# A decoder layer in split fp32: inputs stored back to front, and the two halves of each weight side by side

## The chip, the cores and the metric

The kernel runs on one core of one Trainium2 chip. The metric is device time in microseconds (us), the median of the runs shown; three runs of the kernel before gave 2773.8, 2774.07 and 2774.15 us.

## What is computed

One layer of a hybrid recurrent decoder, for 256 prompt tokens and 32 sample tokens (8 sequences of 4) together, so T = 288 columns in every product. Cut to what matters here:

```
h    = rmsnorm(x)
proj = h @ w_in                      # 2048 -> z | xBC | dt | q | f | i | g | gates
y_a  = grouped_rmsnorm(ssd(conv(xBC), dt) * silu(z)) @ w_br_a      # 4096 -> 2048
y_b  = (rmsnorm(hgrn2(q, f, i)) * silu(g)) @ w_br_b                # 2048 -> 2048
x    = x + rmsnorm((sigmoid(ga) * y_a + sigmoid(gb) * y_b) @ w_out)
x    = x + rmsnorm(relu(rmsnorm(x) @ w_up)^2 @ w_down)             # 2048 -> 8192 -> 2048
x    = x + sigmoid(rmsnorm(x) @ w_ple_gate) * (p @ w_ple_proj)
```

All is in fp32. The outputs are x and the new recurrent and convolution states.

## The kernel before

Everything stands with features on the 128 partitions and the 288 tokens along the free axis. The weights of all large products come from DRAM as 772 slabs of 512 KB in the order in which they are used. A slab is 8 blocks of 128x128 (SK = 8): one output tile of 128 features, and 8 of the 128-feature tiles of the input.

A slab passes four stations. SyncE loads it into one of four slots of `raw` (RING = 4). ScalarE rounds it to the reduced-precision type fp32r into `w_hi` (`split_hi`, L508). VectorE subtracts what was rounded from the whole and puts the rest into `w_lo` (`split_lo`, L1024). TensorE then multiplies (`multiply`, L1665 to L1667): for each of the 8 blocks three matmuls of 288 columns, w_hi with the input's high part, w_hi with its low part, and w_lo with its high part, all summed in one PSUM bank. So a slab is 24 matmuls, each with its own load of a 128x128 weight block. `multiply_pair` (L1681 to L1683) does the same for two output tiles at once where a normalised input is only just being made, and the loop at L2065 to L2067 for the small projection of p.

The splits run three slabs ahead of the matmuls (AHEAD = 3): calls of `ahead` stand between the other instructions of ScalarE and VectorE, by hand, one for each slab that TensorE multiplies. The waits are: ScalarE for the load (`raw_in`) and for the slot to be free of matmuls (`slab_used`), VectorE for `hi_done`, TensorE for `lo_done`, and SyncE's next load into the slot for `lo_done`.

Each input of a product is split in the same way, one or several tiles of 288 columns at a time, into fp32r tiles: h_hi and h_lo (the normalised x, made three times: L533 and L1061, then twice L889 and L1515), o (L633, L1239), y (L801, L1452), m (L826, L1464), u (L897, L1564) and p (L958, L1605). A tile is 1152 bytes of each partition, and the tiles of an input follow one another. The buffers h_hi, o_hi, y_hi, u_hi and m_hi start 480 bytes past a multiple of 512 (`aligned` does this for the first four).

The stages in order, with their slabs: HGRN, 16 heads of 8 slabs (128); the branch projection with its gate (64); SSD, 8 groups of 20 slabs (160); the other branch projection with its gate (96); the output product (32); the feed-forward (256); the last projection and gate (4 and 32). In HGRN and SSD, TensorE, VectorE and ScalarE also have the recurrences to do, between the slabs. In HGRN, `level` gives views of two halves of pairs at seven distances: for distance 1 its operands take every second element.

Lines of the prediction's steps: L1190, L1191, L1216 and L1217 (VectorE on views of `level`), L1146 and L1150 (a product and a reduction in HGRN, once a head; the reduction steps over 64 elements), L1411 (once a group of SSD), L1941 (TensorE, 128-column products in SSD).

```
raw = sb("raw", [P, RING, SK, P])
w_hi = sb("w_hi", [P, RING, SK, P], F32R)
w_lo = sb("w_lo", [P, RING, SK, P], F32R)
...
        for h in LEVELS:                                     # 64, 32, 16, 8, 4, 2, 1
            c4 = level(hcum, 0, h)                           # "p (b a j) -> p b a j", a=2, j=h
            e4 = level(he, LOFF[h], h)
            ...
            V.tensor_tensor(e4[:, :, 1, :], c4[:, :, 1, :], ref, ALU.subtract)
            V.tensor_tensor(e4[:, :, 0, :], ref, c4[:, :, 0, :], ALU.subtract)
```

Of the kernel before, what the change touches and what calls it, by code (L numbers as in the profile page):

```python
# [30 lines left out]
P = 128  # L31
# [115 lines left out]
def layer_program(nc, io):  # L147
# [353 lines left out]
    def _(act):  # L501
        def split_hi(m, k):

            act.wait_ge(raw_in[k], (m + 1) * 16)
            if not (isinstance(m, int) and m == 0):

                act.wait_ge(slab_used, m * RING + (k + 1 - RING))
            nc.scalar.activation(w_hi[:, k], raw[:, k], ACT.Copy).then_inc(hi_done, 1)  # L508

# [21 lines left out]
        for c in range(NC):  # L531
            act.wait_ge(n_xn, 2 * c + 2)
            nc.scalar.activation(h_hi[:, 2 * c:2 * c + 2], hn32[:, 2 * c:2 * c + 2],  # L533
                                 ACT.Copy).then_inc(n_hi, 1)
            if c in (1, 4):
                split_hi(0, (c + 2) // 3)
# [34 lines left out]
        def hgrn(it, first, gemm):  # L571
# [60 lines left out]
            if not first:  # L632
                nc.scalar.activation(tile_at(o_hi, r), one(hso[:, :]), ACT.Copy).then_inc(hg_ohi, 1)  # L633
            nxt(7)
# [165 lines left out]
        def y_hi_chunk(c):  # L800
            nc.scalar.activation(y_hi[:, 4 * c:4 * c + 4], y32[:, 4 * c:4 * c + 4], ACT.Copy).then_inc(y_his, 1)  # L801

# [21 lines left out]
        def merged_hi(t):  # L824
            act.wait_ge(ga_m, t + 1)
            nc.scalar.activation(tile_at(m_hi, t), one(aya[:, :]), ACT.Copy, scale=0.5).then_inc(ga_hi, 1)  # L826

# [67 lines left out]
        def up_hi_part(t, tt):  # L895
            act.wait_ge(up_sq, tt + 1)
            nc.scalar.activation(tile_at(u_hi, t), one(tmp[:, :]), ACT.Copy).then_inc(up_hi, 1)  # L897

# [58 lines left out]
        act.wait_ge(p_land, 16)  # L957
        nc.scalar.activation(p_hi[:, :, :], p_in[:, :, :], ACT.Copy).then_inc(p_his, 1)  # L958
        down(0, True, 1)
# [58 lines left out]
    def _(dve):  # L1018
        V = nc.vector

        def split_lo(m, k):

            dve.wait_ge(hi_done, m * RING + (k + 1))
            V.tensor_tensor(w_lo[:, k], raw[:, k], w_hi[:, k].bitcast(F32), ALU.subtract).then_inc(lo_done, 1)  # L1024

# [33 lines left out]
        def normalised_lo(c):  # L1059
            dve.wait_ge(n_hi, c + 1)  # L1060
            V.tensor_tensor(h_lo[:, 2 * c:2 * c + 2], hn32[:, 2 * c:2 * c + 2],  # L1061
                            h_hi[:, 2 * c:2 * c + 2].bitcast(F32), ALU.subtract).then_inc(n_lo, 1)
# [69 lines left out]
        def hgrn(it, first, gemm):  # L1132
# [104 lines left out]
            if not first:  # L1237
                dve.wait_ge(hg_ohi, it)
                V.tensor_tensor(tile_at(o_lo, it - 1), one(hso[:, :]), tile_at(o_hi, it - 1).bitcast(F32),  # L1239
                                ALU.subtract).then_inc(hg_olo, 1)  # L1240
# [209 lines left out]
        for c in range(8):  # L1450
            dve.wait_ge(y_his, c + 1)
            V.tensor_tensor(y_lo[:, 4 * c:4 * c + 4], y32[:, 4 * c:4 * c + 4],  # L1452
                            y_hi[:, 4 * c:4 * c + 4].bitcast(F32), ALU.subtract).then_inc(y_los, 1)
            if c in (1, 3):
                ahead(U_GA, 2 * GA_SLABS, 0, 6 + c // 2)

        def merge(t):
            dve.wait_ge(evac, t * 2 + (T_GA + 2))
            dve.wait_ge(ga_in, t * 16 + 16)
            V.scalar_tensor_tensor(aya[:, :], atg[:, :], 1.0, aya[:, :], ALU.add, ALU.mult).then_inc(ga_t, 1)  # L1460
            dve.wait_ge(ga_t, t + 1)
            V.tensor_tensor(aya[:, :], aya[:, :], amb[:, :], ALU.add).then_inc(ga_m, 1)
            dve.wait_ge(ga_hi, t + 1)
            V.scalar_tensor_tensor(tile_at(m_lo, t), one(aya[:, :]), 0.5, tile_at(m_hi, t).bitcast(F32),  # L1464
                                   ALU.mult, ALU.subtract).then_inc(ga_lo, 1)
# [91 lines left out]
        def up_tile(t, j, half):  # L1557
# [5 lines left out]
            dve.wait_ge(up_hi, tt + 1)  # L1563
            V.tensor_tensor(tile_at(u_lo, t), one(tmp[:, :]), tile_at(u_hi, t).bitcast(F32),  # L1564
                            ALU.subtract).then_inc(up_lo, 1)
# [38 lines left out]
        dve.wait_ge(p_his, 1)  # L1604
        V.tensor_tensor(p_lo[:, :, :], p_in[:, :, :], p_hi[:, :, :].bitcast(F32), ALU.subtract).then_inc(p_los, 1)  # L1605
        down(0, True, 1)
# [48 lines left out]
    def _(pe):  # L1655
        M = nc.tensor

        def multiply(m, k, out, hi, lo, kt0, first, last, chunks=None):


            pe.wait_ge(lo_done, m * RING + (k + 1))
            for i in range(SK):
                if chunks is not None and i % chunks[1] == 0:
                    pe.wait_ge(chunks[0], (kt0 + i) // chunks[1] + 1)
                M.matmul(out, w_hi[:, k, i], hi[:, kt0 + i], start=first and i == 0, stop=False)  # L1665
                M.matmul(out, w_hi[:, k, i], lo[:, kt0 + i], start=False, stop=False)  # L1666
                op = M.matmul(out, w_lo[:, k, i], hi[:, kt0 + i], start=False, stop=last and i == SK - 1)  # L1667
            op.then_inc(slab_used, 1)

        def multiply_pair(fu, s0, kt0, first, last, banks, chunk0):  # L1670
# [6 lines left out]
            for i in range(SK):  # L1677
                if i % 2 == 0:
                    pe.wait_ge(n_lo, chunk0 + (kt0 + i) // 2 + 1)
                for k, out in zip(slots, (banks[0][:, 0:T], banks[1][:, 0:T])):  # L1680
                    M.matmul(out, w_hi[:, k, i], h_hi[:, kt0 + i], start=first and i == 0, stop=False)  # L1681
                    M.matmul(out, w_hi[:, k, i], h_lo[:, kt0 + i], start=False, stop=False)
                    op = M.matmul(out, w_lo[:, k, i], h_hi[:, kt0 + i], start=False, stop=last and i == SK - 1)  # L1683
                    if i == SK - 1:
# [367 lines left out]
        for s in range(4):  # L2052
            m, k = slab(U_PROJ, 4, 0, s)
            pe.wait_ge(lo_done, m * RING + k + 1)
            for j in range(4):
# [7 lines left out]
                for i in range(2):  # L2063
                    w = 2 * j + i
                    M.matmul(out, w_hi[:, k, w], p_hi[:, i], start=i == 0, stop=False)  # L2065
                    M.matmul(out, w_hi[:, k, w], p_lo[:, i], start=False, stop=False)
                    op = M.matmul(out, w_lo[:, k, w], p_hi[:, i], start=False, stop=i == 1)  # L2067
                op.then_inc(pj_tile if j < 3 else slab_used, 1)
# [250 lines left out]
```

## Time and profile before

| what | value |
|---|---|
| median of three runs | 2774.07 us (2773.8 to 2774.15) |
| span of the profiled execution | 2770.1 us, 4.0 us under the median; its own whole time is not listed |
| PE (TensorE matmul) busy | 2709.0 us, 98% |
| DVE (VectorE) busy | 1787.1 us, 65% |
| ACT (ScalarE) busy | 1421.8 us, 51% |
| POOL (GpSimd) busy | 182.9 us, 7% |
| DMA | 484.22 MB, mean 175 GB/s |

The span runs from the first instruction to the last. Engines work side by side, so the busy times don't add up. Matmuls are pipelined and the end of each is modelled, so records of neighbouring matmuls overlap: the distance between starts tells the pace, not the length of one. PEld is TensorE's loading of weights, which overlaps the matmul before it. "Chain" is the chain of work that ended last, followed back from the last instruction. PEclk is the granted TensorE clock, 1.00 for 2.4 GHz and 0.50 for 1.2 GHz.

### The profile page before, as it was taken

What the parts mean: (1) busy time and instruction counts of PE and PEld (TensorE: products, weight loads), DVE (VectorE), ACT (ScalarE), POOL (GpSimd) and SP (SyncE); (2) the same over time, 40 slices, a digit from 0 to 9 for tenths busy, and PEclk for the clock granted to TensorE, in tenths of its full rate; (3) what the DMA queues carried; (4) which work ended last, traced back from release to release, by engine and by line L of the source; (5) the groups of instructions that cost most, each with busy time, mean ns of one, the idle gap of its engine ahead of it and who ended that gap; (6) DMA issues with size and microseconds to landing.
All of it is one profiled execution on the core that took longest, in us unless ns stands there. A gap on an engine that the chain in (4) does not pass through costs nothing.

```text
span 2770.1 us, 59417 instructions
## 1 busy us (share of the span) xinstructions
PE 2709.0 (98%) x22077; PEld 2639.3 (95%) x22077; DVE 1787.1 (65%) x3214; ACT 1421.8 (51%) x2285; POOL 182.9 (7%) x297
## 2 busy tenths in 40 slices
PE   6999999999999999999989999989999999999999
PEld 5999999999999999999989999989999999999989
DVE  7878787844378888888864444476543355654475
ACT  6666666643356556556643334454443344444363
POOL 0111111100011111111110000000000000000000
PEclk9999999999999999999999999999999999999999
DMA  4544454555556665665555556435554455554544
GB/s 170 176 161 161 163 175 157 165 179 177 172 203 207 199 209 200 210 204 202 191 174 179 174 169 209 164 119 175 164 173 165 162 166 167 164 170 162 165 132 160
DMA packets 135289, 484.22 MB, mean 175 GB/s; under 512 B 17248, under 2 KB 19696, under 8 KB 134080
## 3 DMA queue, kind: packets, MB, share of 16 engines
q1 hardware_dynamic: 114560, 410.88, 44.3%
q0 software_dynamic: 20672, 72.55, 8.2%
q8 instruction: 40, 0.66, 0.1%
q14 instruction: 17, 0.14, 0.0%
HBM read 449.58 MB, written 33.78 MB: 174 GB/s over the span
## 4 chain that ended last, share of the span: by engine, by line
PE 84%; DVE 9%; ACT 3%; issue 2%; DMA 1%; DVEq 0%; POOL 0%; ACTq 0%; POOLq 0%
PE acc L1667 25%; PE acc L1665 25%; PE acc L1666 24%; DVE w_lo L1024 2%; DVE ccv L1310 1%; ACT w_hi L508 1%; PE bank L1665 1%; PE bank L1667 1%; PE bank L1666 1%; PE bank L1846 1%; PE bank L1954 1%; PE bank L1778 1%; PE bank L1941 1%; PE bank L1863 0%; DVE x L1509 0%
## 5 line engine op out<-in xcount | busy, mean ns | idle before, releaser
L1024 DVE TENSOR_TENSOR w_lo<-raw,w_hi 128x1024 fp32r<-128x1024 f32 x772 | 937.9, 1223 | 604.2 <-ACT w_hi L508 599.3
L1665 PE MATMUL acc<-h_hi,w_hi 128*128 128x288 f32 x3872 | 1157.6, 299 | 11.7 <-DVE h_lo L1061 7.7
L1667 PE MATMUL acc<-h_hi,w_lo 128*128 128x288 f32 x3872 | 1148.4, 297 | 0.0
L1666 PE MATMUL acc<-h_lo,w_hi 128*128 128x288 f32 x3872 | 1131.1, 292 | 0.0
L508 ACT ACTIVATE w_hi<-raw 128x1024 fp32r<-128x1024 f32 x772 | 810.8, 1055 | 438.8 <-PE acc L1667 366.2
L1665 PEld LDWEIGHTS acc<-h_hi,w_hi 128*128 128x128 f32 x3872 | 728.5, 188 | 19.7 <-issue 7.4
L1666 PEld LDWEIGHTS acc<-h_lo,w_hi 128*128 128x128 f32 x3872 | 738.8, 191 | 2.8
L1667 PEld LDWEIGHTS acc<-h_hi,w_lo 128*128 128x128 f32 x3872 | 727.1, 188 | 0.0
L1667 PE MATMUL acc<-u_hi,w_lo 128*128 128x288 f32 x1024 | 303.6, 296 | 0.0
L1665 PE MATMUL acc<-u_hi,w_hi 128*128 128x288 f32 x1024 | 302.6, 296 | 0.0
L1666 PE MATMUL acc<-u_lo,w_hi 128*128 128x288 f32 x1024 | 298.5, 292 | 0.0
L1666 PEld LDWEIGHTS acc<-u_lo,w_hi 128*128 128x128 f32 x1024 | 195.2, 191 | 0.0
L1665 PEld LDWEIGHTS acc<-u_hi,w_hi 128*128 128x128 f32 x1024 | 192.4, 188 | 0.0
L1667 PEld LDWEIGHTS acc<-u_hi,w_lo 128*128 128x128 f32 x1024 | 191.8, 187 | 0.0
L1667 PE MATMUL acc<-y_hi,w_lo 128*128 128x288 f32 x384 | 113.9, 296 | 0.0
L1665 PE MATMUL acc<-y_hi,w_hi 128*128 128x288 f32 x384 | 113.5, 296 | 0.0
L1666 PE MATMUL acc<-y_lo,w_hi 128*128 128x288 f32 x384 | 111.9, 292 | 0.0
L1310 DVE SCALAR_TENSOR_TENSOR ccv<-craw,prh,ccv 128x312 f32<-128x312 f32 x144 | 78.3, 544 | 5.1
L1667 PE MATMUL acc<-m_hi,w_lo 128*128 128x288 f32 x256 | 75.9, 296 | 0.0
L1665 PE MATMUL acc<-m_hi,w_hi 128*128 128x288 f32 x256 | 75.6, 296 | 0.0
L1666 PE MATMUL acc<-m_lo,w_hi 128*128 128x288 f32 x256 | 74.6, 292 | 0.0
L1666 PEld LDWEIGHTS acc<-y_lo,w_hi 128*128 128x128 f32 x384 | 73.2, 191 | 0.0
(411 smaller groups left out, 3538.1 us busy)
## 6 DMA issues: line engine op xcount, KB each, us to landing
raw<-in_w SPq DMA_DIRECT2D x772, 512.0 KB, 3.3
ht<-in_ht POOLq DMA_DIRECT2D x64, 256.0 KB, 4.1
out_ssm_s<-ht POOLq DMA_DIRECT2D x64, 256.0 KB, 4.0
cbc<-cum_d POOLq DMA_DIRECT2D x8, 1152.0 KB, 6.8
hs<-in_s POOLq DMA_DIRECT2D x16, 512.0 KB, 4.6
out_hg_s<-hsn POOLq DMA_DIRECT2D x16, 512.0 KB, 5.0
x_in<-in_x SPq DMA_DIRECT2D x4, 576.0 KB, 5.9
mixb<-bmb POOLq DMA_DIRECT2D x16, 144.0 KB, 2.0
```

The source lines that it names most:

```text
L508: nc.scalar.activation(w_hi[:, k], raw[:, k], ACT.Copy).then_inc(hi_done, 1)
L1024: V.tensor_tensor(w_lo[:, k], raw[:, k], w_hi[:, k].bitcast(F32), ALU.subtract).then_inc(lo_done, 1)
L1310: op = V.scalar_tensor_tensor(ccv[:, 0:CVC], src[:, w:w + CVC], prh[:, c, w:w + 1], ccv[:, 0:CVC], ALU.mult, ALU.add)
L1665: M.matmul(out, w_hi[:, k, i], hi[:, kt0 + i], start=first and i == 0, stop=False)
L1666: M.matmul(out, w_hi[:, k, i], lo[:, kt0 + i], start=False, stop=False)
L1667: op = M.matmul(out, w_lo[:, k, i], hi[:, kt0 + i], start=False, stop=last and i == SK - 1)
L1778: M.matmul(b_diag[32 * q:32 * q + 32, 64 * n + 32 * b:64 * n + 32 * b + 32], ks, qs, start=True, stop=True)
L1846: op = M.matmul(bank[5][TS * b:TS * b + TS, :], cfd[:, TS * seq:TS * seq + TS], ht[:, b], start=half == 0, stop=True, skip_group_check=True)
L1941: op = M.matmul(bank[1][:, P * p:P * p + P], xw[:, b, P * p:P * p + P], bt[:, b], start=b == 0, stop=b == 1)
L1954: M.matmul(y[lo:lo + HD, 0:TP], xd[:, 0, HD * j:HD * j + HD], me[:, j, 0:TP], start=True, stop=True)
```

## The change

The high and low parts of a weight stand next to each other in one buffer, `w_split`: for each block of 128x128 the 128 columns follow at a step of two elements (8 bytes), high parts on the even places and low parts on the odd ones. The buffer takes the place of `w_hi` and `w_lo` and has their size together. Every split input tile is written with its 288 columns in the opposite order: the splits read their source from the last column to the first. The matmuls read these tiles from the last column to the first, so the products come out in the order that they had. No instruction is added or taken away, and no wait changes.

```diff
-    w_hi = sb("w_hi", [P, RING, SK, P], F32R)
-    w_lo = sb("w_lo", [P, RING, SK, P], F32R)
+    SLOT = 2 * SK * P
+    w_split = sb("w_split", [P, RING * SLOT], F32R)
+
+    def slot(k):
+
+        at = k * SLOT
+        return w_split[:, at:at + SLOT].rearrange("p (i n a) -> p i a n", i=SK, a=2)
+
+    w_hi = [slot(k)[:, :, 0] for k in range(RING)]
+    w_lo = [slot(k)[:, :, 1] for k in range(RING)]
...
-            nc.scalar.activation(w_hi[:, k], raw[:, k], ACT.Copy).then_inc(hi_done, 1)
+            nc.scalar.activation(w_hi[k], raw[:, k], ACT.Copy).then_inc(hi_done, 1)
...
-            V.tensor_tensor(w_lo[:, k], raw[:, k], w_hi[:, k].bitcast(F32), ALU.subtract).then_inc(lo_done, 1)
+            V.tensor_tensor(w_lo[k], raw[:, k], w_hi[k].bitcast(F32), ALU.subtract).then_inc(lo_done, 1)
...
-                op = nc.scalar.activation(h_hi[:, t], x2[:, t], ACT.Identity, scale=cols[:, col + t:col + t + 1])
+                op = nc.scalar.activation(h_hi[:, t], x2[:, t, ::-1], ACT.Identity, scale=cols[:, col + t:col + t + 1])
...
-                op = V.scalar_tensor_tensor(h_lo[:, t], x2[:, t], cols[:, col + t:col + t + 1],
+                op = V.scalar_tensor_tensor(h_lo[:, t], x2[:, t, ::-1], cols[:, col + t:col + t + 1],
...
-                M.matmul(out, w_hi[:, k, i], hi[:, kt0 + i], start=first and i == 0, stop=False)
-                M.matmul(out, w_hi[:, k, i], lo[:, kt0 + i], start=False, stop=False)
-                op = M.matmul(out, w_lo[:, k, i], hi[:, kt0 + i], start=False, stop=last and i == SK - 1)
+                M.matmul(out, w_hi[k][:, i], hi[:, kt0 + i, ::-1], start=first and i == 0, stop=False)
+                M.matmul(out, w_hi[k][:, i], lo[:, kt0 + i, ::-1], start=False, stop=False)
+                op = M.matmul(out, w_lo[k][:, i], hi[:, kt0 + i, ::-1], start=False, stop=last and i == SK - 1)
```

The other splits of inputs (o, y, m, u, p and the first h) and the matmuls of `multiply_pair` and of the small projection are changed in the same way.

## Rows read from the trace of the kernel before

**Rows 1.** The page: busy time by engine, and the chain by engine

```profile
PE 2709.0 (98%) x22077; PEld 2639.3 (95%) x22077; DVE 1787.1 (65%) x3214; ACT 1421.8 (51%) x2285; POOL 182.9 (7%) x297
...
PE 84%; DVE 9%; ACT 3%; issue 2%; DMA 1%; DVEq 0%; POOL 0%; ACTq 0%; POOLq 0%
```

**Rows 2.** The page's costliest groups: out<-in, shapes, xcount | busy us, mean ns | idle before

```profile
L1024 DVE TENSOR_TENSOR w_lo<-raw,w_hi 128x1024 fp32r<-128x1024 f32 x772 | 937.9, 1223 | 604.2 <-ACT w_hi L508 599.3
...
L508 ACT ACTIVATE w_hi<-raw 128x1024 fp32r<-128x1024 f32 x772 | 810.8, 1055 | 438.8 <-PE acc L1667 366.2
```

**Rows 3.** Waits of all engines: who <- whom, us in total, times, longest

```profile
DVE w_lo L1024 <- ACT w_hi L508: 599.3, 487, 2.8
ACT w_hi L508 <- PE acc L1667: 366.2, 232, 3.5
```

**Rows 4.** Busy time by stretch: us, PE, PEld, DVE, ACT, POOL (x instructions), PEclk, DMA, GB/s

```profile
60.00:460.00 400.00, 398.98 (x4378) 381.37 (x4378) 323.69 (x940) 268.09 (x452) 44.75 (x49) 1.00 0.49 166
...
700.00:1400.00 700.00, 691.90 (x5287) 656.59 (x5286) 551.97 (x1011) 405.06 (x834) 104.02 (x190) 1.00 0.60 200
```

**Rows 5.** Busy time by stretch, one of the feed-forward, where TensorE does slabs alone

```profile
2200.00:2400.00 200.00, 200.00 (x1515) 200.00 (x1514) 111.15 (x138) 88.04 (x117) 0.00 (x0) 1.00 0.51 165
```

**Rows 6.** Busy time by stretch, the first matmuls of the feed-forward

```profile
1823.82:1825.97 2.15, 2.15 (x10) 2.15 (x10) 2.12 (x5) 0.96 (x2) 0.00 (x0) 0.50 0.00 0
```

**Rows 7.** Timeline of PE in that stretch: start us, us, engine line operation

```profile
1823.82 0.44 PE L1682 MATMUL acc<-h_lo,w_hi 128*128 128x288 f32 x1
1824.06 0.44 PE L1683 MATMUL acc<-h_hi,w_lo 128*128 128x288 f32 x1
1824.30 0.44 PE L1681 MATMUL acc<-h_hi,w_hi 128*128 128x288 f32 x1
1824.54 0.44 PE L1682 MATMUL acc<-h_lo,w_hi 128*128 128x288 f32 x1
```

**Rows 8.** Timeline of PE in the output product: the first matmul of four tiles

```profile
1801.63 0.29 PE L1665 MATMUL acc<-m_hi,w_hi 128*128 128x288 f32 x1
...
1802.02 0.30 PE L1665 MATMUL acc<-m_hi,w_hi 128*128 128x288 f32 x1
...
1802.43 0.30 PE L1665 MATMUL acc<-m_hi,w_hi 128*128 128x288 f32 x1
...
1802.83 0.29 PE L1665 MATMUL acc<-m_hi,w_hi 128*128 128x288 f32 x1
```

**Rows 9.** Timeline of PEld in SSD: sixteen weight loads in a row

```profile
1060.00 1.89 PEld L1941 LDWEIGHTS bank<-bt,xw 128*128 128x128 f32 x16
```

**Rows 10.** Timeline of DVE in HGRN: `level` at distance 4, 2 and 1

```profile
113.05 0.28 DVE L1190 TENSOR_TENSOR he<-hcum 128x128 f32<-128x128 f32 x1
...
113.45 0.30 DVE L1190 TENSOR_TENSOR he<-hcum 128x144 f32<-128x144 f32 x1
...
113.89 0.30 DVE L1190 TENSOR_TENSOR he<-hcum 128x144 f32<-128x144 f32 x1
```

**Rows 11.** Timeline of DVE in HGRN: the product, and the reduction that steps over 64

```profile
101.33 0.56 DVE L1146 TENSOR_TENSOR hdm<-bank,consts 128x384 f32<-128x384 f32 x1
...
102.08 0.86 DVE L1150 TENSOR_REDUCE hab<-hdm 128x64 f32<-128x384 f32 x1
```

**Rows 12.** Groups by line and shape: the input splits at a norm

```profile
L889 ACT ACTIVATE h_hi<-x,cols 128x288 fp32r<-128x288 f32 x32 | 15.5, 539 | 18.0 <-DVE x L1509 18.0
...
L1515 DVE SCALAR_TENSOR_TENSOR h_lo<-x,cols,h_hi 128x288 fp32r<-128x288 f32 x32 | 15.1, 511 | 0.3 <-ACT h_hi L889 0.3
```

**Rows 13.** The chain by line, in HGRN (60 to 460 us)

```profile
by line: PE acc L1665 26.5%; PE acc L1667 26.1%; PE acc L1666 25.5%; PE bank L1778 3.1%; PE bank L1758 1.9%; PE bank L1765 1.7%; PE bank L1807 1.5%; PE bank L1771 1.4%; PE bank L1769 1.2%; PE bank L1797 1.0%; PE bank L1796 1.0%; PE bank L17
```

**Rows 14.** The chain by line, in SSD (700 to 1400 us)

```profile
by line: PE acc L1665 17.9%; PE acc L1667 17.4%; PE acc L1666 17.0%; issue 6.9%; DVE ccv L1310 5.4%; DVE w_lo L1024 4.7%; ACT w_hi L508 3.2%; PE bank L1954 2.3%; PE bank L1846 2.1%; PE bank L1941 2.0%; DVE ccv L1306 1.6%; ACT me L721 1.6%; 
```

**Rows 15.** Two lines' instructions: count, ns min/median/max, first and last start us

```profile
L1150 DVE TENSOR_REDUCE hab<-hdm x16: 847/856/859, 70.7 to 550.8; 128x64 f32<-128x384 f32 x16
...
L1411 DVE TENSOR_TENSOR cbm<-bank,consts x8: 557/557/559, 796.6 to 1353.1; 128x384 f32<-128x384 f32 x8
```

More of the change, by code:

```diff
@@ L532, in _ @@
             act.wait_ge(n_xn, 2 * c + 2)
-            nc.scalar.activation(h_hi[:, 2 * c:2 * c + 2], hn32[:, 2 * c:2 * c + 2],
+            nc.scalar.activation(h_hi[:, 2 * c:2 * c + 2], hn32[:, 2 * c:2 * c + 2, ::-1],
                                  ACT.Copy).then_inc(n_hi, 1)
@@ L632, in hgrn @@
             if not first:
-                nc.scalar.activation(tile_at(o_hi, r), one(hso[:, :]), ACT.Copy).then_inc(hg_ohi, 1)
+                nc.scalar.activation(tile_at(o_hi, r), one(hso[:, ::-1]), ACT.Copy).then_inc(hg_ohi, 1)
             nxt(7)
@@ L825, in merged_hi @@
             act.wait_ge(ga_m, t + 1)
-            nc.scalar.activation(tile_at(m_hi, t), one(aya[:, :]), ACT.Copy, scale=0.5).then_inc(ga_hi, 1)
+            nc.scalar.activation(tile_at(m_hi, t), one(aya[:, ::-1]), ACT.Copy, scale=0.5).then_inc(ga_hi, 1)
         for t in range(EARLY):
@@ L896, in up_hi_part @@
             act.wait_ge(up_sq, tt + 1)
-            nc.scalar.activation(tile_at(u_hi, t), one(tmp[:, :]), ACT.Copy).then_inc(up_hi, 1)
+            nc.scalar.activation(tile_at(u_hi, t), one(tmp[:, ::-1]), ACT.Copy).then_inc(up_hi, 1)
         def up(i, half, banks, done=0):
@@ L957, in _ @@
         act.wait_ge(p_land, 16)
-        nc.scalar.activation(p_hi[:, :, :], p_in[:, :, :], ACT.Copy).then_inc(p_his, 1)
+        nc.scalar.activation(p_hi[:, :, :], p_in[:, :, ::-1], ACT.Copy).then_inc(p_his, 1)
         down(0, True, 1)
@@ L1238, in hgrn @@
                 dve.wait_ge(hg_ohi, it)
-                V.tensor_tensor(tile_at(o_lo, it - 1), one(hso[:, :]), tile_at(o_hi, it - 1).bitcast(F32),
+                V.tensor_tensor(tile_at(o_lo, it - 1), one(hso[:, ::-1]), tile_at(o_hi, it - 1).bitcast(F32),
                                 ALU.subtract).then_inc(hg_olo, 1)
@@ L1463, in merge @@
             dve.wait_ge(ga_hi, t + 1)
-            V.scalar_tensor_tensor(tile_at(m_lo, t), one(aya[:, :]), 0.5, tile_at(m_hi, t).bitcast(F32),
+            V.scalar_tensor_tensor(tile_at(m_lo, t), one(aya[:, ::-1]), 0.5, tile_at(m_hi, t).bitcast(F32),
                                    ALU.mult, ALU.subtract).then_inc(ga_lo, 1)
@@ L1563, in up_tile @@
             dve.wait_ge(up_hi, tt + 1)
-            V.tensor_tensor(tile_at(u_lo, t), one(tmp[:, :]), tile_at(u_hi, t).bitcast(F32),
+            V.tensor_tensor(tile_at(u_lo, t), one(tmp[:, ::-1]), tile_at(u_hi, t).bitcast(F32),
                             ALU.subtract).then_inc(up_lo, 1)
@@ L1680, in multiply_pair @@
                 for k, out in zip(slots, (banks[0][:, 0:T], banks[1][:, 0:T])):
-                    M.matmul(out, w_hi[:, k, i], h_hi[:, kt0 + i], start=first and i == 0, stop=False)
-                    M.matmul(out, w_hi[:, k, i], h_lo[:, kt0 + i], start=False, stop=False)
-                    op = M.matmul(out, w_lo[:, k, i], h_hi[:, kt0 + i], start=False, stop=last and i == SK - 1)
+                    M.matmul(out, w_hi[k][:, i], h_hi[:, kt0 + i, ::-1], start=first and i == 0, stop=False)
+                    M.matmul(out, w_hi[k][:, i], h_lo[:, kt0 + i, ::-1], start=False, stop=False)
+                    op = M.matmul(out, w_lo[k][:, i], h_hi[:, kt0 + i, ::-1], start=False, stop=last and i == SK - 1)
                     if i == SK - 1:
@@ L2064, in _ @@
                     w = 2 * j + i
-                    M.matmul(out, w_hi[:, k, w], p_hi[:, i], start=i == 0, stop=False)
-                    M.matmul(out, w_hi[:, k, w], p_lo[:, i], start=False, stop=False)
-                    op = M.matmul(out, w_lo[:, k, w], p_hi[:, i], start=False, stop=i == 1)
+                    M.matmul(out, w_hi[k][:, w], p_hi[:, i, ::-1], start=i == 0, stop=False)
+                    M.matmul(out, w_hi[k][:, w], p_lo[:, i, ::-1], start=False, stop=False)
+                    op = M.matmul(out, w_lo[k][:, w], p_hi[:, i, ::-1], start=False, stop=i == 1)
                 op.then_inc(pj_tile if j < 3 else slab_used, 1)
```

8 lines of the change are left out of this document (4 added, 4 removed).

## The prediction

> **What bounds the kernel now.** The page first: TensorE's matmuls fill 98% of the span, VectorE 65%, ScalarE 51%, and the chain that ended last is 84% TensorE [rows 1]. Then the waits: VectorE's low split waits 599.3 us for ScalarE's high split, and that waits 366.2 us for matmuls to free a slot of the ring [rows 3]. So the splits stand ready and are held back by TensorE, not the other way round. By stretch: in the feed-forward TensorE does nothing but slabs, and VectorE is busy for 111 of 200 us [rows 5]. In HGRN VectorE is busy for 323.69 of 400 us, 81%, and in SSD for 551.97 of 700 us, 79% [rows 4]. There TensorE's work is still nearly the whole, but VectorE has only a fifth to spare.
>
> The pace of one matmul is the number that this change is about. In the feed-forward 1515 matmuls take 200.00 us: 132.0 ns each, with the granted clock at 1.00, its upper level of 2.4 GHz [rows 5]. The same instruction at the lower level, 1.2 GHz (granted 0.50), after TensorE had waited for the norm, starts every 0.24 us [rows 6, 7], three steps of exactly 0.72 us in all. That is 288 columns at one in a cycle, with nothing on top. Twice the clock should give 120 ns. So at full clock 12.0 ns of each matmul are spent on something that half the clock doesn't show: not an instruction's fixed cost in cycles, but data that come too late. Nor is the loss even: of three neighbouring tiles of the same product, three matmuls each, one takes 0.39, one 0.41 and one 0.40 us [rows 8], though only the place of the tile differs.
>
> What else reads then is the next weight block. Sixteen loads in a row take 1.89 us, of which the last 0.19 is one load's length; so a load follows a load in (1.89 - 0.19)/15 = 113 ns [rows 9]. While TensorE reads a tile of 1152 bytes in 120 to 132 ns, about 9 bytes a ns, it reads 512 bytes of weights in 113 ns, 4.5 bytes a ns. The inputs overtake the weights in the same memory several times in each matmul, and where the two readers want the same part of it, one waits. That is my reading; the rows show the loss, its dependence on pace and on place, not the cause.
>
> **The change, part by part.**
>
> Weights interleaved: a block now covers 1024 bytes for each part, so in the same 113 ns the weight reader walks at 1024/113 = 9.1 bytes a ns, as fast as the inputs. Inputs reversed and read downwards: both readers go the same way if the weights of a block are read from the last column to the first. Two readers of one speed and one direction keep their distance: they meet at the start at most, one gives way, and they don't meet again. No row shows the direction in which weights are read, so this is the step that decides.
>
> The gain per matmul has ends far apart. The best is all of 12.0 ns [rows 5, 7]. The other end is a loss: twice the bytes swept by the weight reader without the lock, twice the meetings, 12.0 ns more. I take 7 ns, a pace of 125: nearer to the 120 of half clock, since equal speeds are what the two edits together make, and short of it, since each load and each matmul starts anew.
>
> There are 772 splits [rows 2], so 772 slabs of 24 matmuls, 18,528.
> - 484 slabs lie outside HGRN and SSD, where TensorE sets the pace alone: 484 x 24 x 7 ns = 81.3 us.
> - HGRN, 128 slabs: 21.5 us. The three lines of slab matmuls are 78% of the chain there [rows 13], the rest mostly other matmuls, and VectorE's 81% would become 85%. I count nine tenths: 19.4 us.
> - SSD, 160 slabs: 26.9 us. The slab matmuls are only 52% of the chain, with VectorE's and ScalarE's lines between [rows 14]. I count six tenths, 16.1 us; what is late next there is VectorE's convolution and split.
>
> Sum: 117 us less.
>
> The splits, at a step of two elements: VectorE reads one operand and writes its result so, 772 times, 1.223 us each [rows 2]. `level` at distance 1 takes every second element in all three operands: 144 columns in 0.30 us, as at distance 2, where they come in pairs, and 128 columns in 0.28 [rows 10]. The difference of 0.02 us is that of 16 more columns. So the step costs nothing; this is nearly the form of the split, and I take 0. The upper end is a far step: 384 columns at a step of 64 take 0.86 us against 0.56 for a product of 384 [rows 11], 0.78 ns more a column, 0.80 us a split. ScalarE's high split (1.055 us [rows 2]) writes at that step, which no ScalarE row shows; bounds 0 and the same 0.80 us, no gain, since as many elements pass. I take 0, by the nearer row. What covers a small excess on either is the lead of three slabs, 3 x 24 x 132 ns = 9.5 us; it is gone where VectorE has no fifth to spare.
>
> The Vector Engine (DVE) Microarchitecture Reference of the Trainium skill (5.2, Measured stream behaviour on trn2) speaks against this edit: a port keeps its full rate only while its elements come in adjacent pairs. By that rule the split would lose its rate, and the sum would be that of the third rival below. The `level` rows disagree at this step, and they decide.
>
> The reversed reads: 178 tiles are split once each on ScalarE and VectorE, 0.54 and 0.51 us where a norm makes them [rows 12]. No row reads downwards. I take 0, as many bytes in the same order of lines; the upper end is 0.78 ns x 288 = 0.22 us a tile. For the 48 tiles of the three norms, where TensorE waits, that would be 2 x 48 x 0.22 = 21 us; the other 130 lie beside matmuls.
>
> No instruction, DMA or wait is added, and the queues of SP and POOL issue what they did. Faster slabs ask for loads sooner: 165 GB/s and half of the DMA engines' time [rows 5] become 174, which the 200 of SSD [rows 4] covers.
>
> So the span goes from 2770.1 to about 2653 us. With the 4.0 us by which the median stands above it, **2657 us**.
>
> **The rivals.**
> 1. **Twice the meetings (slower).** If weights are read upwards, or the parts of memory that collide are such that two equal streams stay together, the weight reader sweeps twice the bytes and the loss doubles: +12.0 ns x 18,528 = +222 us, 2996; with half of that, 2885. For it: 12 ns are lost already with a slow weight reader. Against: the speeds become equal. It decides on the slab matmuls, from a pace of 132.3 ns (0.3 ns x 18,528 = 5.6 us, 0.2%).
> 2. **The load becomes the bound (slower).** A step of 8 bytes may stretch the load itself. From 132/113 = 1.17 times its time it sets the pace. At 1.3 times, 147 ns: +15 x 18,528 = +278 us, 3052; at twice, 226 ns, over 4500. Against: the matmul reads twice as many columns in a ns as a load does.
> 3. **The splits become the bound (slower).** A head of HGRN takes (550.8 - 70.7)/15 = 32.0 us, a group of SSD (1353.1 - 796.6)/7 = 79.5 [rows 15]. With 0.80 us more a split, VectorE has 81% of 32.0 + 8 x 0.80 = 32.3 us of work a head, and 79% of 79.5 + 20 x 0.80 = 78.8 a group. At 95% busy that takes 34.0 and 82.9 us: 16 x 2.0 + 8 x 3.4 = 59 us more, 2833. Against: rows 10.
> 4. **No meeting at all (same).** If the 12 ns come from the input's read alone, its order and the weights' place change nothing: 2774. For it: no row shows a matmul at full clock without a load beside it. TensorE: Matmul & The Clock Gate of the Trainium skill (Part 2, step 1) says just this: two independent read ports, so loading weights takes nothing from the running matmul. It also states a pace of N/2.4 + 2.5 ns, 122.5 here; the trace has 132.0, so something that page leaves out is at work.
>
> That the change doesn't do what it says I leave out: each read and write follows from the views in the diff.
>
> **How the numbers follow.** My forecast, a gain of 7 ns or some other part of the 12: 0.65. The fourth rival and what comes out even: 0.10. Twice the meetings 0.17, the load 0.04, the splits 0.04: 0.25 together. If all 12 ns go, the same weights give 139 + 33 + 28 = 200 us, 2574. Within the forecast most lies from 2590 up, down to small gains. The range 2590 to 2850 leaves out the last bit of gain (0.05) and the slower cases beyond half of a doubling (0.14). Its likeliest part, the forecast's own, is 2590 to 2740. Faster by over 0.2% (about what a measurement of this kernel can tell from no change) 0.65, within it 0.10, slower 0.25.
>
> **What would show it.** Right: in the feed-forward 200 us hold some 1600 matmuls instead of 1515 at the same granted clock, neighbouring tiles differ by less, the splits stay at 1.223 and 1.055 us, and ScalarE waits less for a slot. The chain in SSD moves from slab matmuls to VectorE. Wrong: a pace above 132 ns (first rival), a weight load above its 0.19 us (second), a split near 2 us with TensorE waiting for `lo_done` (third), or a pace still at 132 (fourth).

## The result, and the profile after

The changed kernel takes 2780.8 us (median of 10 runs, 2778.9 to 2783.2) against 2773.8 us for the kernel before on the same chip: 1.0026 times as long, with a 95% interval of 1.0018 to 1.0035. That is slower by just over what a measurement can tell from no change. The profiled execution spans 2777.0 us against 2770.1.

First the page (busy time by engine, the chain by engine) and the two splits among the costliest groups, of the changed kernel:

```profile
PE 2710.8 (98%) x22077; PEld 2639.6 (95%) x22077; DVE 1790.3 (64%) x3214; ACT 1510.0 (54%) x2285; POOL 182.7 (7%) x297
...
PE 88%; DVE 6%; ACT 3%; issue 1%; DMA 1%; POOL 0%; DVEq 0%; ACTq 0%; POOLq 0%
...
L1032 DVE TENSOR_TENSOR w_split<-raw,w_split 128x1024 fp32r<-128x1024 f32 x772 | 941.0, 1226 | 627.8 <-ACT w_split L516 623.6
...
L516 ACT ACTIVATE w_split<-raw 128x1024 fp32r<-128x1024 f32 x772 | 904.0, 1179 | 405.6 <-PE acc L1675 336.8
```

Only one engine's work has grown: ScalarE's, from 1421.8 to 1510.0 us [rows 1]. It is the high split, 1.179 us where it was 1.055 [rows 2], 772 times 0.124 us. VectorE's split is unchanged: 1.226 us against 1.223, although it reads one operand and writes at a step of two.

Then busy time by stretch (us, PE, PEld, DVE, ACT and POOL with their instructions, granted clock, DMA share, GB/s), one stretch of the feed-forward and the whole of SSD:

```profile
2200.00:2400.00 200.00, 200.00 (x1514) 200.00 (x1514) 109.84 (x135) 95.73 (x116) 0.00 (x0) 1.00 0.51 165
700.00:1400.00 700.00, 688.21 (x5245) 651.20 (x5244) 546.50 (x1003) 419.66 (x832) 101.63 (x185) 1.00 0.59 198
```

The pace, the number the prediction was about, hasn't moved: 1514 matmuls in 200 us, where it was 1515 [rows 5]. (A stretch counts the two matmuls that its edges cut, so I take 2 off from here on: 200/1513 = 132.2 ns before, 200/1512 = 132.3 after. From first to last start in that stretch it is 132.22 ns in both kernels, and 12.2 ns over the 120, not 12.0.) SSD does 42 matmuls fewer in 700 us than before [rows 4].

Yet the change did something to the matmuls. This is TensorE's timeline in the output product, the first matmul of five neighbouring tiles:

```profile
1809.15 0.30 PE L1673 MATMUL acc<-m_hi,w_split 128*128 128x288 f32 x1
...
1809.55 0.30 PE L1673 MATMUL acc<-m_hi,w_split 128*128 128x288 f32 x1
...
1809.94 0.30 PE L1673 MATMUL acc<-m_hi,w_split 128*128 128x288 f32 x1
...
1810.34 0.30 PE L1673 MATMUL acc<-m_hi,w_split 128*128 128x288 f32 x1
...
1810.74 0.30 PE L1673 MATMUL acc<-m_hi,w_split 128*128 128x288 f32 x1
```

The tiles take 0.40, 0.39, 0.40 and 0.40 us, where they took 0.39, 0.41 and 0.40 [rows 8]. In the trace's starts, which are kept to the ns, every tile now has the same three steps, 135, 131 and 131 ns; before, steps ran from 127 to 138 and depended on the tile. The unevenness went, as forecast, if not for the forecast's reason alone (e11_few below). The mean stayed.

Last, one product of SSD that is made once a group (count, shortest, median and longest ns, first and last start):

```profile
L1419 DVE TENSOR_TENSOR cbm<-bank,consts x8: 557/558/558, 797.4 to 1359.0; 128x384 f32<-128x384 f32 x8
```

Before it ran from 796.6 to 1353.1 [rows 15]. So of the 6.9 us by which the span grew, 0.8 had come when this product of SSD's first group was reached, 5.1 came between the first and the last, and 1.0 behind it.

So there are two questions: what holds the pace at 132 ns whatever the layout, and what SSD lost.

### The profile page after: what moved, and what is told of

It is laid out like the page before. It is cut to its first block, busy times and chain, and to the rows that moved or that the text cites. A ratio compares the mean times of both kernels' runs of the same rounds, so it can differ in the third digit from the quotient of the medians.

```text
span 2777.0 us, 59417 instructions
## 1 busy us (share of the span) xinstructions
PE 2710.8 (98%) x22077; PEld 2639.6 (95%) x22077; DVE 1790.3 (64%) x3214; ACT 1510.0 (54%) x2285; POOL 182.7 (7%) x297
## 4 chain that ended last, share of the span: by engine, by line
PE 88%; DVE 6%; ACT 3%; issue 1%; DMA 1%; POOL 0%; DVEq 0%; ACTq 0%; POOLq 0%
PE acc L1673 26%; PE acc L1674 26%; PE acc L1675 25%; DVE w_split L1032 1%; ACT w_split L516 1%; PE bank L1673 1%; PE bank L1674 1%; PE bank L1675 1%; DVE ccv L1318 1%; PE bank L1962 1%; PE bank L1871 1%; PE bank L1786 1%; PE bank L1854 1%; PE bank L1949 1%; PE bank L1912 0%
## 5 line engine op out<-in xcount | busy, mean ns | idle before, releaser
L1032 DVE TENSOR_TENSOR w_split<-raw,w_split 128x1024 fp32r<-128x1024 f32 x772 | 941.0, 1226 | 627.8 <-ACT w_split L516 623.6
L1673 PE MATMUL acc<-h_hi,w_split 128*128 128x288 f32 x3872 | 1163.4, 300 | 12.0 <-DVE h_lo L1069 7.3
L1674 PE MATMUL acc<-h_lo,w_split 128*128 128x288 f32 x3872 | 1143.7, 295 | 0.0
L1675 PE MATMUL acc<-h_hi,w_split 128*128 128x288 f32 x3872 | 1143.7, 295 | 0.0
L516 ACT ACTIVATE w_split<-raw 128x1024 fp32r<-128x1024 f32 x772 | 904.0, 1179 | 405.6 <-PE acc L1675 336.8
L1673 PEld LDWEIGHTS acc<-h_hi,w_split 128*128 128x128 f32 x3872 | 754.2, 195 | 20.2 <-issue 6.7
L1674 PEld LDWEIGHTS acc<-h_lo,w_split 128*128 128x128 f32 x3872 | 754.8, 195 | 2.5
L1675 PEld LDWEIGHTS acc<-h_hi,w_split 128*128 128x128 f32 x3872 | 750.8, 194 | 0.0
L1673 PE MATMUL acc<-u_hi,w_split 128*128 128x288 f32 x1024 | 304.1, 297 | 0.0
L1674 PE MATMUL acc<-u_lo,w_split 128*128 128x288 f32 x1024 | 302.1, 295 | 0.0
L1675 PE MATMUL acc<-u_hi,w_split 128*128 128x288 f32 x1024 | 302.1, 295 | 0.0
L1673 PEld LDWEIGHTS acc<-u_hi,w_split 128*128 128x128 f32 x1024 | 199.2, 194 | 0.0
L1675 PEld LDWEIGHTS acc<-u_hi,w_split 128*128 128x128 f32 x1024 | 198.1, 194 | 0.0
L1673 PE MATMUL acc<-y_hi,w_split 128*128 128x288 f32 x384 | 114.0, 297 | 0.0
L1675 PE MATMUL acc<-y_hi,w_split 128*128 128x288 f32 x384 | 113.3, 295 | 0.0
```

What stands on the lines that cost most here:

```text
L516: nc.scalar.activation(w_hi[k], raw[:, k], ACT.Copy).then_inc(hi_done, 1)
L1032: V.tensor_tensor(w_lo[k], raw[:, k], w_hi[k].bitcast(F32), ALU.subtract).then_inc(lo_done, 1)
L1673: M.matmul(out, w_hi[k][:, i], hi[:, kt0 + i, ::-1], start=first and i == 0, stop=False)
L1674: M.matmul(out, w_hi[k][:, i], lo[:, kt0 + i, ::-1], start=False, stop=False)
L1675: op = M.matmul(out, w_lo[k][:, i], hi[:, kt0 + i, ::-1], start=False, stop=last and i == SK - 1)
```

## The experiments

**Either edit alone.** e1_inter takes the reversal back and e2_rev the interleaving:

```diff
 e1_inter, on the changed kernel, at every split and slab matmul:
-M.matmul(out, w_hi[k][:, i], hi[:, kt0 + i, ::-1], ...)
+M.matmul(out, w_hi[k][:, i], hi[:, kt0 + i], ...)
 e2_rev, on the changed kernel, in slot(k):
-rearrange("p (i n a) -> p i a n", i=SK, a=2)
+rearrange("p (a i n) -> p i a n", i=SK, a=2)
```

> Interleaved weights alone: the split inputs stay written upwards and are read upwards. Theory A (mine, from the prediction: the 12 ns over 120 ns are spent where the two readers meet, and the layout moves the meetings): the weight reader and the input reader now run against each other in step, and the slab matmuls' mean distance moves away from 132.2 ns, by at least 2 ns either way. Theory B (the excess has nothing to do with where the operands lie): the mean stays within 0.3 ns of 132.2 ns whatever pattern the single distances show; the ScalarE split takes about 1.18 us as in the changed kernel and the time is that of the changed kernel, about 2780 us. Rival for the 7 us lost: if the reversed reads cost them, this kernel stands at about 2774 us with the ScalarE split still at 1.18 us.

> Reversed inputs alone: the high and low weights lie in runs again, one slab's high part behind the other. Theory A: as the readers run in opposite directions at different speeds, they meet more often or less, and the mean distance moves by at least 2 ns. Theory B: mean distance within 0.3 ns of 132.2 ns, ScalarE split back at 1.055 us, time that of the kernel before, about 2774 us, because ScalarE's strided write is what cost the 7 us. Rival: the reversed reads cost the 7 us, and the time is about 2780 us with the split at 1.055 us.

e1_inter took 2816.5 us (4 runs), 1.0146 times the kernel before (1.0125 to 1.0168). e2_rev took 2765.8 us (8 runs), 0.9973 times (0.9962 to 0.9983): faster than both kernels. TensorE by stretch (us, busy with matmuls, granted clock, DMA share, GB/s), of e1_inter in the feed-forward and in the last gate product:

```profile
2200.00:2400.00 200.00, 200.00 (x1478) 1.00 0.48 159
2750.00:2790.00 40.00, 40.00 (x305) 1.00 0.52 177
```

The same view of e2_rev, in the feed-forward:

```profile
2200.00:2400.00 200.00, 200.00 (x1521) 1.00 0.50 166
```

The high split among the page's groups, e2_rev:

```profile
L516 ACT ACTIVATE w_split<-raw 128x1024 fp32r<-128x1024 f32 x772 | 809.6, 1053 | 437.9 <-PE acc L1675 388.0
```

And the product of SSD in e2_rev, first and last start:

```profile
L1419 DVE TENSOR_TENSOR cbm<-bank,consts x8: 557/558/558, 796.4 to 1352.6; 128x384 f32<-128x384 f32 x8
```

Theory B falls: the layout moves the pace, to 135.5 ns with the weights interleaved and to 131.7 with the inputs reversed. Theory A, which asked for at least 2 ns either way in both, is met by e1_inter alone: the layout moves the pace by -0.5 to +3.3 ns, nowhere near the 12. And the reversed reads of the splits cost nothing: ScalarE's split is back at 1.053 us, and SSD at 556.2 us from first to last, where it was 556.5.

**The size of the matmul.** e3_cols, on the kernel before:

```diff
-M.matmul(out, w_hi[:, k, i], hi[:, kt0 + i], ...)
+M.matmul(out, w_hi[:, k, i], cut(hi, kt0 + i, n), ...)   n columns from the start of the tile on
```

> The kernel before, with another number of input columns per slab matmul in some stages (output projection 224, up half 0 256, down half 0 320, up half 1 384, down half 1 512, last gate stage 192; the rest 288), so those stages compute something else. Theory A and theory B as a fixed excess (about 12 ns on top of N/2.4 GHz): 105, 119, 145, 172, 225 and 92 ns (the last only if loading 128 weight columns, about 107 ns, is not slower). Theory A as meetings would let the excess grow with N, since a longer read meets the weight reader more often: 4/3 of 12 ns at 384 columns, 16/9 at 512. Theory C (the weight load and a fixed latency behind it set the pace, so 132 ns is not about the columns at all): 132 ns at 224, 256 and 192 too, and growth only above 288.

TensorE by stretch, with 224, 256, 320, 384, 512 and, in the last gate product, 192 columns:

```profile
1730.00:1790.00 60.00, 60.00 (x540) 1.00 0.59 201
1880.00:1980.00 100.00, 100.00 (x843) 1.00 0.56 187
2040.00:2200.00 160.00, 160.00 (x1093) 1.00 0.44 148
2260.00:2460.00 200.00, 200.00 (x1141) 1.00 0.36 123
2540.00:2800.00 260.00, 260.00 (x1116) 1.00 0.27 93
2905.00:2945.00 40.00, 40.00 (x360) 1.00 0.62 197
```

That is 111.5, 118.9, 146.7, 175.6, 233.4 and 111.7 ns. Theory C falls, since 256 columns are faster than 288; at 224 and 192, which take the same, something else holds: the load of the weights (e10_alone below). The excess over N/2.4 isn't fixed either: 12.2 ns at 256 as at 288, then 13.4, 15.6 and 20.1. From 320 to 512 columns a column costs (233.4 - 146.7)/192 = 0.452 ns instead of 0.417, or 4 bytes in 0.452 ns = 8.9 bytes a ns. Theory A's growth with N (16 ns of excess at 384, 21 at 512) fits this about as well; but it now had a rival, an input reader that is itself too slow.

**What the excess needs.** e4_parts, e5_kinds and e6_ways change operands stage by stage in the kernel before. In short, what each puts in place of the weights w, the inputs x and the output:

```diff
 e4_parts
+w[:, 0:32]   w[:, 0:64]                  fewer weight columns, out[0:32], out[0:64]
+out, bank[2], bank[4]                    one bank for each product
+start=True, stop=True                    no accumulation
+w.bitcast(BF16)[:, 1::2], x.bitcast(BF16)[:, 1::2]
 e5_kinds
+x[:, 0:1].to_broadcast([P, T])           one input column 288 times
+w[:, 0:1].to_broadcast([P, P])           one weight column 128 times
+hi.bitcast(BF16)[:, 0:T], [:, 1::2], [:, 0:512]   inputs; the weights w.bitcast(BF16)[:, 1::2] in all three
 e6_ways
+x[:, ::-1]; weights at [::4] or [::2] over neighbouring blocks; inputs at [::2] over two tiles
```

> The kernel before, with one thing changed in each of five stages, so those compute something else or leave products out: output projection loads 32 of 128 weight columns, up half 0 loads 64, down half 0 sends the three products to three PSUM banks and keeps one of them, up half 1 starts every product afresh instead of accumulating, down half 1 takes the upper halves of the operands as bf16. Theory B (a fixed excess of the engine): 132 ns in all of them, with bf16 unknown. Theory C (weight load sets the pace): 32 and 64 columns fall to the 120 ns of the columns or near it. Theory D (the accumulation in one bank costs the 12 ns): three banks or no accumulation fall to near 120 ns while 32 and 64 columns stay at 132. Theory A: fewer weight columns mean fewer meetings, so 64 takes about half the excess off (126 ns) and 32 three quarters (123 ns).

> The kernel before, one thing changed in each of five stages, whose products are then others or are sent to a bank that nobody reads. From the runs so far the distance of two fp32 matmuls is about 3 ns plus 0.45 ns a column (118.9 at 256 columns, 175.5 at 384, 233.4 at 512), and the layouts move it only from 131.65 to 135.7 ns. Theory E (the input reader delivers at most one 4-byte column each 0.45 ns, by bytes): one column read 288 times is still 4 bytes each, 132 ns; bf16 in a row halves the bytes and gives 120 to 124 ns, and 512 such columns 213 to 218 ns; bf16 elements 4 bytes apart stay near the 127.8 ns measured before; the same weight 128 times stays at about 131 ns. Theory F (the engine takes a column each 0.45 ns, whatever is read): 132 ns for bf16 in a row too and 233 ns at 512. Theory A (readers getting in each other's way in SBUF): one column read 288 times, or one weight 128 times, touches one place only, and goes to 120 ns or near it.

> The kernel before with the operands read in another way in each of five stages, which then compute something else: output projection inputs downwards; up half 0 weights 16 bytes apart, inputs upwards; down half 0 weights 16 bytes apart, inputs downwards; up half 1 inputs 8 bytes apart; down half 1 weights 8 bytes apart, inputs upwards. If the way the two readers run against each other is what remains of theory A, inputs downwards alone give 131.7 ns again, weights 8 bytes apart with inputs upwards 132.2 or 135.7 ns, and 16 bytes apart more than that upwards, no more than 132.3 ns downwards; inputs 8 bytes apart double the bytes passed and lie above 132.2 ns. If the 0.57 ns of the reversed kernel came from elsewhere in it (the splits' reads, where the buffers lie), inputs downwards here stay at 132.2 ns.

TensorE by stretch in e4_parts: 32 weight columns, 64 weight columns, three banks, no accumulation, bf16 elements 4 bytes apart:

```profile
1730.00:1810.00 80.00, 80.00 (x615) 1.00 0.51 170
1890.00:2030.00 140.00, 140.00 (x1064) 1.00 0.50 167
2060.00:2220.00 160.00, 160.00 (x1212) 1.00 0.48 165
2260.00:2420.00 160.00, 160.00 (x1212) 1.00 0.51 166
2480.00:2620.00 140.00, 140.00 (x1097) 1.00 0.51 169
```

In e5_kinds: one input column, bf16 in a row, bf16 4 bytes apart, one weight column:

```profile
1730.00:1800.00 70.00, 70.00 (x574) 1.00 0.54 180
1870.00:2010.00 140.00, 140.00 (x1145) 1.00 0.56 180
2060.00:2200.00 140.00, 140.00 (x1098) 1.00 0.52 172
2240.00:2400.00 160.00, 160.00 (x1233) 1.00 0.51 166
```

From its timeline (start us, us), two matmuls on 512 columns of bf16 in a row, six matmuls apart:

```profile
2518.74 0.38 PE L1684 MATMUL bank<-u_hi,w_lo 128*128 128x512 bf16 x1
...
2520.03 0.38 PE L1684 MATMUL bank<-u_hi,w_lo 128*128 128x512 bf16 x1
```

In e6_ways: inputs downwards; weights 16 bytes apart with inputs upwards, then downwards; inputs 8 bytes apart; weights 8 bytes apart:

```profile
1730.00:1800.00 70.00, 70.00 (x533) 1.00 0.49 167
1880.00:2140.00 260.00, 260.00 (x1116) 1.00 0.28 93
2200.00:2480.00 280.00, 280.00 (x1202) 1.00 0.28 93
2520.00:2870.00 350.00, 350.00 (x1366) 1.00 0.26 85
2920.00:3080.00 160.00, 160.00 (x1212) 1.00 0.51 165
```

| what is read in one matmul of 288 columns | ns |
|---|---|
| kernel before | 132.2 |
| three banks; no accumulation | 132.2; 132.2 |
| 64 or 32 weight columns | 131.8; 130.5 |
| one weight column, 128 times | 130.0 |
| one input column, 288 times | 122.4 |
| bf16 in a row; 4 bytes apart | 122.5; 127.7 |
| inputs downwards | 131.8 |
| inputs 8 bytes apart | 256.6 |
| weights 8 or 16 bytes apart | 132.2; 233.4 |

Theory D falls: the banks don't matter. The excess needs moving input bytes. With one input column 122.4 ns are left, 2.4 over the 120, though a whole weight block is loaded beside it. With half the bytes it is the same 122.5, and 512 bf16 columns take (2520.03 - 2518.74)/6 = 215 ns. At 8 bytes apart 2304 bytes are passed in 256.6 ns: 9.0 bytes a ns, close to the 8.9 of e3_cols, so what counts is the memory passed over, not only the elements used. Theory F falls. Theory E is right for bf16, and wrong in its first row: one column read 288 times was to take 132 ns, and theory A said 120 or near it. So the limit looks to be on bytes of memory passed, not on bytes handed over. It is not clean in another row: bf16 elements 4 bytes apart pass as many bytes as fp32 and take 127.7 (beside bf16 weights), not 132. And taking the weight reader off, as far as one column 128 times does that, saves only 2.2 ns; a half or three quarters of the weight columns left out give 0.4 and 1.7 ns, where theory A asked for 6 and 9. Inputs downwards pace here as in e2_rev (131.67 ns from start to start in both), so nothing else in that kernel makes its gain. Weights 16 bytes apart were to be slow in one direction alone; they are in both, for a reason of their own (below).

**How much the layout could give.** e7_shift is the changed kernel, and e9_revshift e2_rev, with the four weight slots moved by 0, 32, 64 and 96 bytes:

```diff
-        at = k * SLOT
+        at = k * SLOT + 8 * k
```

> The changed kernel with the four weight slots moved by 0, 32, 64 and 96 bytes against the inputs. If readers that run side by side at one speed either stay clear of each other or stay in each other's way (what the change was argued by), the distance depends on the slot: one of the four falls to the 120 ns of the columns or at least below 131.6 ns, another rises. If the pace is set inside the engine or by the input reader alone, all four keep 132.2 to 132.3 ns and the time stays at about 2780 us.

> The kernel with reversed inputs alone, its four weight slots moved by 0, 32, 64 and 96 bytes against the inputs. Between the two readers only 2.3 ns are left to be had: 132.2 ns with both moving, 129.9 with the weight reader on one address, 122.5 with the input reader on one column. If the place of their meetings decides within these, the slots spread over 130 to 133 ns and the best is below 131.65; if only the directions count, all four slots stay at 131.65 to 131.8 ns and the time at 2766 us.

e7_shift took 2785.6 us (5 runs; 1.0028 to 1.0057 times the kernel before), e9_revshift 2777.6 (10 runs; 1.0006 to 1.0025). The timeline of e9_revshift has the same matmul, the fourth, of five slabs in a row, in slots 1, 2, 3, 0 and 1:

```profile
2245.22 0.30 PE L1673 MATMUL acc<-h_hi,w_split 128*128 128x288 f32 x1
...
2248.41 0.30 PE L1673 MATMUL acc<-h_hi,w_split 128*128 128x288 f32 x1
...
2251.58 0.30 PE L1673 MATMUL acc<-h_hi,w_split 128*128 128x288 f32 x1
...
2254.78 0.30 PE L1673 MATMUL acc<-h_hi,w_split 128*128 128x288 f32 x1
...
2257.93 0.30 PE L1673 MATMUL acc<-h_hi,w_split 128*128 128x288 f32 x1
```

Slabs take 3.15 to 3.20 us, in the starts 131.7 ns a matmul in slot 0, which hasn't moved, and 133.3, 131.9 and 133.1 in the others: place decides, within 1.7 ns, and no slot lies below 131.65. In e7_shift the slots run from 132.0 to 133.2. Neither expectation of either run came out in full: the slots differ, and none falls below 131.6. None goes near 120, as two readers that keep clear of each other were to.

**Each reader by itself.** In short, the stages of e10_alone and e11_few, in the kernel before:

```diff
 e10_alone: x[:, ::-1] with one weight column; weights at [::2] with 192 columns; weights at [::4],
 then at [::2], with one input column; 192 columns
 e11_few: w[:, 0:2], out[0:2] with x, then x[:, ::-1]; w[:, 0:32] with x[:, ::-1];
 w[:, 64:65].to_broadcast([P, P]) with x, then x[:, ::-1]
```

> The kernel before with each reader taken by itself in five stages, which then compute something else: output projection inputs downwards with one weight 128 times; up half 0 weights 8 bytes apart and 192 columns; down half 0 weights 16 bytes apart and one input column 288 times; up half 1 weights 8 bytes apart and one input column; down half 1 192 columns. If the 7.4 ns between one input column (122.5) and one weight (129.9) are the input reader's own pace, reading downwards changes nothing: 129.9 ns; if they are a direction's, it falls. If a weight load by itself goes by the bytes it passes (233.3 ns at 16 bytes apart is 8.8 bytes a ns), 16 bytes apart takes 233 ns again with one input column, and 8 bytes apart 117 ns: hidden behind 288 columns (122.5 ns with one input column) and bare at 192 columns, where it shows as 117 to 122 ns against 111.7 ns for the weights in a row.

> The kernel before with next to no weights read in five stages, which then compute something else: output projection two of 128 weight columns, inputs upwards; up half 0 two weight columns, inputs downwards; down half 0 32 weight columns, inputs downwards; up half 1 weight column 64 read 128 times, inputs upwards; down half 1 the same with inputs downwards. Reading I (the input reader alone is slower downwards, and the changed kernel, with the same steps of 135, 131 and 131 ns as inputs downwards beside one weight, has no meetings left but pays them back there): two columns downwards give 132.3 ns, upwards 129.9 ns or less, and column 64 the same pair. Reading II (one weight read 128 times is an obstacle of its own, which the input reader meets in one place or another): two columns give one and the same value both ways, at or below 130 ns, and column 64 another pair than column 0.

TensorE by stretch, the stages in that order, in e10_alone and then e11_few:

```profile
1730.00:1810.00 80.00, 80.00 (x608) 1.00 0.50 168
1890.00:2010.00 120.00, 120.00 (x1011) 1.00 0.58 184
2060.00:2340.00 280.00, 280.00 (x1202) 1.00 0.29 94
2380.00:2540.00 160.00, 160.00 (x1309) 1.00 0.54 177
2600.00:2700.00 100.00, 100.00 (x898) 1.00 0.65 197
```

```profile
1730.00:1800.00 70.00, 70.00 (x541) 1.00 0.52 171
1890.00:2010.00 120.00, 120.00 (x910) 1.00 0.52 166
2060.00:2220.00 160.00, 160.00 (x1213) 1.00 0.49 164
2260.00:2420.00 160.00, 160.00 (x1233) 1.00 0.53 170
2480.00:2620.00 140.00, 140.00 (x1061) 1.00 0.51 165
```

This is the answer to the first question. With only two weight columns read, a matmul takes 129.9 ns with its inputs upwards and 132.2 with its inputs downwards; one weight column, the first or the one at index 64, gives the same pair (130.0 up; 132.0 and 132.2 down), though before e10_alone one weight column had been expected to stay at 129.9 downwards or to fall. 32 weight columns downwards give 132.1. Reading I holds. And the steps of two columns downwards are 135, 131 and 131 ns on every tile: those of the changed kernel. So in the changed kernel the weight reader leaves no trace in the times that I can see, as the change meant. Its inputs alone take as long downwards as inputs and weights together took before. Upwards, two weight columns still leave neighbouring tiles uneven, 0.387 and 0.393 us in turn (0.391 to 0.403 before): so part of the unevenness was the input reader's own, and reading downwards takes that part away.

By itself a load of 128 weights shows at 192 columns: 111.6 ns in a row, 118.9 at 8 bytes apart, and at 16 bytes apart 233.3 whatever the inputs do. There 2048 bytes in 233.3 ns are 8.8 bytes a ns, and 1024 in 118.9 are 8.6: a load at a step, too, goes by about the bytes that it passes, at nearly the inputs' 8.9. In a row, 512 bytes in 111.6 ns, something else holds it.

**ScalarE's split.** e8_halves has the layout of before and a longer high split:

```diff
-nc.scalar.activation(w_hi[:, k], raw[:, k], ACT.Copy).then_inc(hi_done, 1)
+nc.scalar.activation(w_hi[:, k, 0:SK // 2], raw[:, k, 0:SK // 2], ACT.Copy)
+nc.scalar.activation(w_hi[:, k, SK // 2:], raw[:, k, SK // 2:], ACT.Copy).then_inc(hi_done, 1)
```

> The kernel before with each high split on ScalarE written as two halves, which lengthens it by one instruction's fixed part, some 0.2 us a split (0.124 us in the changed kernel), with the layout as before. If a longer ScalarE split is what the changed kernel lost in its SSD stage (about 5.6 us of waits between slabs 192 and 352, 160 splits), this one loses there 8 to 10 us, little elsewhere, and stands at about 2783 us with 132.2 ns a matmul. If the loss came from something else of the interleaving or reversal, the time stays within 2 us of 2773 us.

It took 2781.2 us (10 runs), 1.0027 times the kernel before (1.0017 to 1.0037). Its two halves among the page's groups:

```profile
L508 ACT ACTIVATE w_hi<-raw 128x512 fp32r<-128x512 f32 x772 | 483.4, 626 | 413.7 <-PE acc L1668 343.1
L509 ACT ACTIVATE w_hi<-raw 128x512 fp32r<-128x512 f32 x772 | 477.2, 618 | 0.0
```

The first of its waits (us in total, times, longest):

```profile
DVE w_lo L1025 <- ACT w_hi L509: 622.4, 509, 2.9
```

And the product of SSD:

```profile
L1412 DVE TENSOR_TENSOR cbm<-bank,consts x8: 558/558/558, 797.4 to 1360.4; 128x384 f32<-128x384 f32 x8
```

626 + 618 ns are 0.19 us more than 1.055. SSD takes 563.0 us from its first group to its last, 6.5 more than before, at an unchanged pace; the changed kernel lost 5.1 there, and its low split waits 623.6 us for the high one, as here (622.4), not 599.3 [rows 3]. That is less than the 8 to 10 us expected, so the loss isn't in proportion to the split's length, but a longer split alone brings it about.

## Why the prediction was wrong

The kernel came out 0.26% slower where 0.65 stood for faster by over 0.2%. 2780.8 lies inside the range, but far from 2657.

- **The bound** was right: TensorE at full clock, its slab matmuls one behind the other.
- **"12.0 ns of each matmul are spent on ... data that come too late"** was right for four fifths of them. The argument from half clock was to exclude a fixed cost; but with one input column, where no new bytes come, 2.4 ns stay, and bf16 keeps 2.5 at 288 columns and (215.8 in the starts) at 512: a cost of each matmul that half clock didn't show either. **The step that failed is the next one, that the inputs "overtake the weights ... several times in each matmul", and with it the term of 7 ns.** The 12 ns (12.2 by the count above) are three things: 2.4 that stay with one input column (122.4); 7.5 that the input reader needs by itself (129.9 with two weight columns); and 2.3 that the weight reader adds (132.2). Only the last was to be had from the weights' place: 2.3 x 18,528 = 43 us at most, not 117. The uneven tiles [rows 8] came from there in part, and they did vanish; but a difference that depends on place says nothing of how much of a loss depends on place. The warning stood in the prediction: 9 bytes a ns for the inputs, against 4 x 2.4 = 9.6 that full clock asks for.
- **Reading downwards** had no price in the matmul, only in the splits. It costs 132.2 - 129.9 = 2.3 ns beside next to no weights, which pays back just what clearing the weight reader away gains. By this account the time is so near to no change because the two cancel; that they come out equal is luck as far as the runs show, and the prices don't simply add: with the weights in a row, reading downwards gained 0.5 ns (e2_rev), and interleaving on top of it lost that again.
- **The fourth rival** came nearest, with 0.10: "the input's read alone". But its "order and the weights' place change nothing" isn't so: the order costs 2.3 ns beside two weight columns, and either edit alone moves the pace (135.5 and 131.7). TensorE: Matmul & The Clock Gate of the Trainium skill (Part 1, "Wait — 56ns, not 53.3ns?") gives N/2.4 + 2.5 ns, an estimate of 122.5 here: one input column (122.4) and bf16 in a row (122.5; 215 at 512) agree, and fp32 columns, whose bytes are held back, don't. The same page of the Trainium skill (Part 2, step 1) has two independent read ports, so that a load takes nothing from the running matmul: that holds here for one input column, not for moving ones, where two weight columns instead of 128 take 2.3 ns off.
- **The second rival's** place is real but far: 8 bytes apart a load takes 118.9/111.6 = 1.07 times as long, short of the 1.17 where it was to decide; at 16 bytes apart it does decide, with 233 ns.
- **The splits.** VectorE's 0 was right (1.226 us). ScalarE's 0 was not: 0.124 us, inside the bounds of 0 to 0.80, for which the prediction had no row. It shows where the prediction said that cover ends, in SSD, and makes most of the 7 us: 5.1 of 6.9. e8_halves shows that a longer split alone does this; the other 1.8 us no run assigns. The reversed reads' 0 was right, by e2_rev.
- **Shares.** HGRN at nine tenths and SSD at six look too high for a small gain, by one profile of each kernel: e2_rev is 0.2 us ahead at SSD's first group and 0.5 at its last. The rest of the 5.7 us by which its span is shorter (2764.4) comes behind SSD: 420 slabs of 24 matmuls there at 0.5 ns make 5.0 us.

## What to carry to other kernels

Before a loss is put down to two readers in each other's way, take each away by itself: one input column, or two weight columns, shows in one run what either is worth. An fp32 operand that streams at TensorE's full clock was held by its own bytes here, 8.9 a ns; none of the places, steps and directions tried mended that, and fewer bytes did. An edit that makes one engine's helper a tenth longer is paid in the stage where two engines hand work to each other, even with half of that engine's time free over the whole.

## What was not expected

- Of the versions run, the fastest is e2_rev, the reversal without the interleaving: 2765.8 us. Why it paces at 131.7 ns, below the 132.2 of downward inputs beside two weight columns, and why downwards is slower at all, stays open.
- One layout can have two paces. e1_inter's gate product reads the same input tiles and the same slots as its feed-forward, at 40/303 = 132.0 ns instead of 135.5; in its starts a slab has 132.2 or 135.5, and keeps it until a wait breaks the row of matmuls.
- Writing 1024 elements at a step of two costs ScalarE 0.124 us in the changed kernel (0.096 in e1_inter, whose split takes 1.151) and VectorE nothing.
